# A fused Griffin-style layer on one core: the sums of weight blocks in the gate and up products are made by accumulating transfers

## The chip, the cores and the metric

One core of a Trainium2 chip runs one launch. The metric is the device time in microseconds. A core has five engines that run on their own and meet at semaphores: TensorE (PE, with its weight loads as PEld), VectorE (DVE), ScalarE (ACT), GpSimd (POOL) and SyncE (SP), which in this kernel issues nearly all transfers between the device memory and the on-chip memory.

## The reference, cut to what matters

The layer normalizes x (512 rows of 2048 values), runs a gated recurrence and a sliding-window attention side by side, merges them, adds a cross attention, and ends with a gated feed-forward part and a final norm. The change is in the feed-forward part:

```python
hf = rmsnorm(x, norm_ffn[l])
x = x + (jax.nn.silu(hf @ w_gate[l]) * (hf @ w_up[l])) @ w_down[l]
```

w_gate and w_up are 2048 x 5632, w_down is 5632 x 2048, all in float32.

## The kernel before, in words

Each float32 product is made of three products of a rounded high part and a rest: low x high, high x low, high x high. Weights are therefore split on the chip: ScalarE copies a raw block to its high part (f_hi, line 1499), and VectorE subtracts it from the raw block to get the low part (f_lo, line 2087; the first four on GpSimd, line 557).

Gate and up are computed together as a 2 x 2 block product in the manner of Strassen and Winograd, with seven products in place of eight. The 2048 values that are summed over are halved, and so are the 512 rows of hf. The two halves of w_gate are the blocks b11 and b21, those of w_up are b12 and b22. For each of 11 groups of 512 columns (n = 0 to 10) the seven products p need these right-hand blocks: b11; b11+b12; b11+b12+b22; b22; b12+b22; b21; b11+b12+b22+b21. A block is 1024 x 512 and is worked in four chunks c of 128 x 1024 elements (512 KB), so a group has 28 chunks and chunk i is 28n + 4p + c. For each chunk TensorE does 24 matmuls (line 568 to 570, or 843 to 845 where the sum of two results is wanted in two accumulators).

The raw blocks live in three sets of four slots, f_raw[0..2][c]. SP loads b11, b12, b22 and b21 (quad_load, line 453), each into the slots of one set; the roles of the sets rotate with n (raw_sets). The sums are made in place by VectorE (f_sum, line 2082): one addition of two whole slots for each chunk of p = 1, 2, 4 and 6, two chunks ahead of its f_low in VectorE's order. The semaphore f_t_added counts them, and ScalarE's f_high waits for it. There are three f_hi and three f_lo buffers: f_high(i) waits until TensorE has done chunk i-3 (f_chunk_done), f_low(i) waits for f_high(i), and TensorE waits for f_low(i) (f_lo_ready).

SP's order in a group: after f_lo of chunk 16+c it loads b21 of this group and b11 of the next; after f_lo of chunk 24+c, b12 and b22 of the next; then the two stores of finished activations (store_act, line 480), which wait for ScalarE. In the last group the first four loads of w_down stand where b11 stood. In group 0, VectorE and ScalarE also make the left-hand operands (operand_steps), in a written order between the f_low and f_high calls, from the transposed rows of hf; b12's slots overlap the buffers of the norm before, so its load waits for row_squared and row_scaled.

GpSimd makes the low parts of all earlier weights (line 545), then f_low(0) to f_low(3), and has nothing after them. After the groups comes the down projection of 88 chunks (w_down), whose raw blocks use the slots of one of the sets.

Of the kernel before, what the change touches and what calls it, by code (L numbers as in the profile page):

```python
# [24 lines left out]
P = 128  # L25
# [25 lines left out]
CK = 8  # L51
RING = 4
# [50 lines left out]
def build_trunk(nc, a, out):  # L103

    ctx = ExitStack()
    with ctx:
# [156 lines left out]
        f_hi_ready, f_lo_ready = S("f_hi_ready"), S("f_lo_ready")  # L263
        f_chunk_done, f_t_added = S("f_chunk_done"), S("f_t_added")

# [4 lines left out]
        def raw_sets(n):  # L270

            return ((0, 1, 2), (2, 0, 1), (1, 2, 0))[n % 3]


        load_of = {}
        slot_loads = {}
        for n in range(NQ):
            a_set, b_set, c_set = raw_sets(n)
            for name, x in (("b11", a_set), ("b12", b_set), ("b22", c_set), ("b21", b_set)):
                for c in range(4):  # L280
                    slot_loads[x, c] = slot_loads.get((x, c), 0) + 1
                    load_of[n, name, c] = (x, c, slot_loads[x, c])
# [5 lines left out]
        raw_in = [[S(f"f_raw_in{x}{c}") for c in range(4)] for x in range(3)]  # L288

# [6 lines left out]
        def split_source(i):  # L296

            if i >= 28 * NQ:
                x, c, _ = load_of["down", i - 28 * NQ]
                return f_raw[x][c]  # L300
            n, r, p, c = step(i)
            a_set, b_set, c_set = raw_sets(n)
            return f_raw[(a_set, a_set, a_set, c_set, b_set, b_set, a_set)[p]][c]

        def sums_to(i):

            n, r, p, c = step(i)
            return 16 * n + sum(4 for q in (1, 2, 4, 6) if q < p) + c + 1

# [17 lines left out]

        w_in = a["w_in"].rearrange("l d n -> (l d) n")

        @block.sync  # L330
        def _(sp):
# [110 lines left out]

            w_gate = a["w_gate"].rearrange("l (k p) n -> p (l k) n", p=P)
            w_up = a["w_up"].rearrange("l (k p) n -> p (l k) n", p=P)
            w_down = a["w_down"].rearrange("l (k p) n -> p (l k) n", p=P)

            def quad_load(n, name, c):

                x, slot, _ = load_of[n, name, c]
                w = w_gate if name in ("b11", "b21") else w_up  # L450
                k0 = 2 * c + (0 if name in ("b11", "b12") else CK)
                dst = f_raw[x][slot][:, :].rearrange("p (k n) -> p k n", n=512)
                sp.dma_start(dst, w[:, k0:k0 + 2, n * 512:(n + 1) * 512]).then_inc(raw_in[x][slot], 16)

# [4 lines left out]
            for c in range(4):  # L459
                sp.wait_ge(w_lo_ready, C_XO + 4 + c + 1)  # L460
                quad_load(0, "b11", c)
# [4 lines left out]
            quad_load(0, "b12", 0)  # L466
            sp.wait_ge(S("row_scaled"), 2 * TT)
            for c in (1, 2, 3):
                quad_load(0, "b12", c)
            sp.wait_ge(S("x2_spilled"), 32)  # L470
            sp.wait_ge(S("x2_spilled_late"), 32)
            for c in range(4):
                quad_load(0, "b22", c)

# [61 lines left out]
        @block.gpsimd  # L536
        def _(pool):
            pool.memset(ones[:, :], 1.0).then_inc(S("ones_set"), 1)

            def split_lo(s, v=0, k=0):  # L540

                slot = s % RING
                before(pool, w_hi_ready, s + 1, v, k)
                before(pool, chunk_done, s - RING + 1, v, k)
                pool.tensor_tensor(w_lo[:, slot], w_raw[:, slot], w_hi[:, slot].bitcast(F32),  # L545
                                   ALU.subtract).then_inc(w_lo_ready, 1)

# [12 lines left out]
            for i in range(4):  # L560
                f_low(i)

        @block.tensor
# [583 lines left out]
        def _(act):  # L1147
# [335 lines left out]
            def f_high(i):  # L1483
# [139 lines left out]
        def _(dve):  # L1623
# [440 lines left out]

            def f_sum(i):

                if i >= 28 * NQ:
                    return
                n, r, p, c = step(i)
                if p not in (1, 2, 4, 6):  # L2070
                    return
                a_set, b_set, c_set = raw_sets(n)
                o, other = {1: (a_set, b_set), 2: (a_set, c_set), 4: (b_set, c_set), 6: (a_set, b_set)}[p]
                for name in {1: ("b11", "b12"), 2: ("b22",), 4: (), 6: ("b21",)}[p]:
                    x, slot, count = load_of[n, name, c]
                    dve.wait_ge(raw_in[x][slot], 16 * count)
                if i < 8:
                    dve.wait_ge(f_lo_ready, i - 3)
                if p in (2, 6):
                    dve.wait_ge(f_t_added, sums_to(i - (4 if p == 2 else 16)))  # L2080
                o = f_raw[o][c][:, :]
# [133 lines left out]
            for i in range(2, 28 * NQ + len(DOWN)):  # L2215
                f_sum(i + 2)
                if i == 4:
# [77 lines left out]
```

## Time and profile before

| | us |
|---|---|
| median of 3 runs | 2931.21 (2930.93 to 2933.22) |
| the profiled execution | 2933.35 |
| its span | 2931.5 |
| TensorE busy in the span | 2870.1 |
| VectorE busy | 1351.9 |
| ScalarE busy | 1141.4 |
| GpSimd busy | 618.3 |

The page of the profile gives sums over a program with different stages, so the busy shares alone don't say what a stage is bound by. The view by windows gives the same sums for one stretch, and the timeline gives single instructions with what they waited for. Matmuls of a busy TensorE start 0.23 us apart; the 0.39 us of one overlap with the next. An instruction that issues a transfer isn't counted as busy.

### The profile page before, as it was taken

How to read it: one execution, taken by the hardware profiler on the slowest of the kernel's cores; microseconds unless marked ns; L12 is line 12 of the kernel's file. 1: busy time of each engine (PE TensorE's matmuls, PEld its weight loads, DVE VectorE, ACT ScalarE, POOL GpSimd, SP SyncE). 2: the span in 40 equal slices, each digit the busy share in tenths (PEclk: the TensorE clock that was granted, in tenths of full speed). 3: DMA queues.
4: the chain of work that ended last, by engine and by line, in shares of the span. 5: the costliest groups of instructions: out<-in, count | busy, mean ns of one | idle time of the engine just before them, and what ended most of it. 6: DMA issues, size and time to landing. Idle time of an engine off the chain costs nothing.

```text
span 2931.5 us, 34896 instructions
## 1 busy us (share of the span) xinstructions
PE 2870.1 (98%) x13685; PEld 2388.8 (81%) x13685; DVE 1351.9 (46%) x1618; ACT 1141.4 (39%) x1487; POOL 618.3 (21%) x257
## 2 busy tenths in 40 slices
PE   8999999999999999999999999999999999999998
PEld 7888878788888888878877888888888888888886
DVE  3354555410034300020427977777777775334333
ACT  6443444412244422232335544444444443223223
POOL 6433333244433344444331000000000000000000
PEclk9999999999999999999999999999999999999999
DMA  7422222233322233342223333333332345434442
GB/s 232 121 73 72 72 72 72 60 95 86 103 77 77 85 90 102 106 151 94 87 94 123 130 130 122 130 122 130 127 105 106 123 140 220 146 137 148 151 144 108
DMA packets 330543, 334.05 MB, mean 114 GB/s; under 512 B 26712, under 2 KB 234928, under 8 KB 327344
## 3 DMA queue, kind: packets, MB, share of 16 engines
q1 hardware_dynamic: 329808, 331.95, 34.4%
q8 instruction: 91, 1.49, 0.2%
q10 hardware_dynamic: 608, 0.32, 0.0%
q14 instruction: 36, 0.29, 0.0%
HBM read 311.25 MB, written 20.97 MB: 113 GB/s over the span
## 4 chain that ended last, share of the span: by engine, by line
PE 77%; DVE 3%; ACT 1%; issue 1%; DMA 0%; ACTq 0%; DVEq 0%; SPq 0%
PE psum L568 19%; PE psum L569 19%; PE psum L570 19%; PE psum L843 5%; PE psum L844 5%; PE psum L845 5%; PE psum L889 1%; PE psum L1076 1%; PE psum L787 0%; DVE f_lo L2087 0%; PE psum L768 0%; DVE f_raw L2082 0%; DVE op_lo L1630 0%; PE psum L941 0%; PE psum L777 0%
## 5 line engine op out<-in xcount | busy, mean ns | idle before, releaser
L545 POOL TENSOR_TENSOR w_lo<-w_raw,w_hi 128x1024 fp32r<-128x1024 f32 x248 | 607.7, 2460 | 932.4 <-ACT w_hi L1153 931.2
L1499 ACT ACTIVATE f_hi<-f_raw 128x1024 fp32r<-128x1024 f32 x396 | 419.7, 1061 | 765.3 <-PE psum L570 502.5
L2087 DVE TENSOR_TENSOR f_lo<-f_raw,f_hi 128x1024 fp32r<-128x1024 f32 x392 | 479.7, 1224 | 472.2 <-ACT f_hi L1499 470.9
L568 PE MATMUL psum<-op_hi,w_lo 128*128 128x512 f32 x1216 | 486.8, 400 | 0.0
L569 PE MATMUL psum<-op_lo,w_hi 128*128 128x512 f32 x1216 | 477.6, 393 | 0.0
L570 PE MATMUL psum<-op_hi,w_hi 128*128 128x512 f32 x1216 | 476.8, 392 | 0.0
L1153 ACT ACTIVATE w_hi<-w_raw 128x1024 fp32r<-128x1024 f32 x248 | 257.7, 1055 | 241.4 <-PE psum L570 222.7
L568 PE MATMUL psum<-f_hi,pa_lo 128*128 128x512 f32 x704 | 274.1, 389 | 0.0
L570 PE MATMUL psum<-f_hi,pa_hi 128*128 128x512 f32 x704 | 273.9, 389 | 0.0
L569 PE MATMUL psum<-f_lo,pa_hi 128*128 128x512 f32 x704 | 273.9, 389 | 0.0
L568 PEld LDWEIGHTS psum<-op_hi,w_lo 128*128 128x128 f32 x1216 | 230.8, 190 | 49.2 <-issue 2.4
L570 PEld LDWEIGHTS psum<-op_hi,w_hi 128*128 128x128 f32 x1216 | 230.7, 190 | 49.2
L569 PEld LDWEIGHTS psum<-op_lo,w_hi 128*128 128x128 f32 x1216 | 230.8, 190 | 47.7 <-issue 1.7
L2082 DVE TENSOR_TENSOR f_raw<-f_raw,f_raw 128x1024 f32<-128x1024 f32 x176 | 215.3, 1224 | 3.6 <-DMA f_raw<-in_w_up 3.6
L568 PEld LDWEIGHTS psum<-f_hi,pa_lo 128*128 128x128 f32 x704 | 132.1, 188 | 27.7
L570 PEld LDWEIGHTS psum<-f_hi,pa_hi 128*128 128x128 f32 x704 | 132.1, 188 | 27.6
L569 PEld LDWEIGHTS psum<-f_lo,pa_hi 128*128 128x128 f32 x704 | 132.1, 188 | 27.1
L568 PE MATMUL psum<-f_hi,a_lo 128*128 128x512 f32 x352 | 137.9, 392 | 0.0
L843 PE MATMUL psum<-f_hi,s_lo 128*128 128x512 f32 x352 | 137.0, 389 | 0.2 <-DVE f_lo L2087 0.2
L570 PE MATMUL psum<-f_hi,a_hi 128*128 128x512 f32 x352 | 137.1, 389 | 0.0
L569 PE MATMUL psum<-f_lo,a_hi 128*128 128x512 f32 x352 | 137.0, 389 | 0.0
L845 PE MATMUL psum<-f_hi,s_hi 128*128 128x512 f32 x352 | 136.9, 389 | 0.0
(308 smaller groups left out, 4447.9 us busy)
## 6 DMA issues: line engine op xcount, KB each, us to landing
w_raw<-in_w_in SPq DMA_DIRECT2D x144, 512.0 KB, 3.8
f_raw<-in_w_gate SPq DMA_DIRECT2D x88, 512.0 KB, 4.6
f_raw<-in_w_up SPq DMA_DIRECT2D x88, 512.0 KB, 5.1
f_raw<-in_w_down SPq DMA_DIRECT2D x88, 512.0 KB, 4.7
pa_raw<-act_scratch SPq DMA_DIRECT2D x44, 512.0 KB, 3.9
w_raw<-in_w_out SPq DMA_DIRECT2D x32, 512.0 KB, 3.7
act_scratch<-c SPq DMA_DIRECT2D x22, 512.0 KB, 3.0
w_raw<-in_w_proj_a SPq DMA_DIRECT2D x16, 512.0 KB, 3.8
```

Of the source, the lines that this page charges most:

```text
L545: pool.tensor_tensor(w_lo[:, slot], w_raw[:, slot], w_hi[:, slot].bitcast(F32), ALU.subtract).then_inc(w_lo_ready, 1)
L568: pe.matmul(b[:, 0:n], wl, xh, start=start, stop=False)
L569: pe.matmul(b[:, 0:n], wh, xl, start=False, stop=False)
L570: return pe.matmul(b[:, 0:n], wh, xh, start=False, stop=stop)
L843: pe.matmul(b, lo[:, kt, f], w[0], start=False, stop=False, skip_group_check=True)
L844: pe.matmul(b, hi[:, kt, f], w[1], start=False, stop=False, skip_group_check=True)
L845: return pe.matmul(b, hi[:, kt, f], w[0], start=False, stop=stop, skip_group_check=True)
L889: last = pe.matmul(bank[4 + j][:, x * P:(x + 1) * P], h_nat[:, t % 2, kt * P:(kt + 1) * P], n_diag[:, t % 2, :], start=True, stop=True)
L1153: act.activation(w_hi[:, slot], w_raw[:, slot], ACT.Copy).then_inc(w_hi_ready, 1)
L1499: act.activation(f_hi[i % FR][:, :], split_source(i)[:, :], ACT.Copy).then_inc(f_hi_ready, 1)
L2082: dve.tensor_tensor(o, o, f_raw[other][c][:, :], ALU.add).then_inc(f_t_added, 1)
L2087: dve.tensor_tensor(f_lo[i % FR][:, :], split_source(i)[:, :], f_hi[i % FR][:, :].bitcast(F32), ALU.subtract).then_inc(f_lo_ready, 1)
```

## The change

f_sum is gone. GpSimd issues, after its four f_low, 16 transfers in each group that read a weight block from the device memory and add it onto what is in the slot (accum_op=ALU.add). Each waits for f_lo of the chunk that used the slot last and for the accumulating transfer before it into the same slot number, and increments raw_added[c]; f_high waits for that. The sequence for one group: b11 is loaded into the first set; b12, b22 and b21 are added onto it, for p = 1, 2, 6. b22 is loaded into the second set and b12 added onto it, for p = 4. b21 is loaded into the third set for p = 5, and that set becomes the first one of the next group, while the first becomes the third. The second set stays. b12 and b22 are thus read more often: a group reads 28 blocks of 512 KB from memory where it read 16. SP loads b22 of the next group after chunk 16+c, b11 of the next after 20+c, and b21 of the next after 24+c. The order of adds in GpSimd's queue is p = 1, 2, 6, 4, four chunks each.

```diff
 def raw_sets(n):
-            return ((0, 1, 2), (2, 0, 1), (1, 2, 0))[n % 3]
+            return ((0, 1, 2), (2, 1, 0))[n % 2]
+        BLOCK = ("b11", "b12", "b22", "b22", "b12", "b21", "b21")
+        ADDS = (1, 2, 6, 4)
...
+            sum_set, low_set, next_set = raw_sets(n)
+            for p, x in ((0, sum_set), (3, low_set), (5, next_set)):
                 for c in range(4):
                     slot_loads[x, c] = slot_loads.get((x, c), 0) + 1
+                    load_of[n, p, c] = (x, c, slot_loads[x, c])
+            for j, p in enumerate(ADDS):
+                for c in range(4):
+                    load_of[n, p, c] = (low_set if p == 4 else sum_set, c, len(ADDS) * n + j + 1)
...
+        raw_in = [w_loaded] + [[S(f"f_raw_in{x}{c}") for c in range(4)] for x in (1, 2)]
+        raw_added = [S(f"f_raw_added{c}") for c in range(4)]
...
+        def up_block(n, p, c):
+            w = w_gate if BLOCK[p] in ("b11", "b21") else w_up
+            k0 = 2 * c + (0 if BLOCK[p] in ("b11", "b12") else CK)
+            return w[:, k0:k0 + 2, n * 512:(n + 1) * 512]
...
+            def quad_load(n, p, c):
+                x, slot, _ = load_of[n, p, c]
+                sp.dma_start(raw_pieces(x, slot), up_block(n, p, c)).then_inc(raw_in[x][slot], 16)
...
             for n in range(NQ):
+                if n < NQ - 1:
+                    for c in range(4):
+                        sp.wait_ge(f_lo_ready, 28 * n + 16 + c + 1)
+                        quad_load(n + 1, 3, c)
                 for c in range(4):
-                    sp.wait_ge(f_lo_ready, 28 * n + 16 + c + 1)
-                    quad_load(n, "b21", c)
+                    sp.wait_ge(f_lo_ready, 28 * n + 20 + c + 1)
                     if n < NQ - 1:
-                        quad_load(n + 1, "b11", c)
+                        quad_load(n + 1, 0, c)
                     else:
                         down_load(c)
                 if n < NQ - 1:
                     for c in range(4):
                         sp.wait_ge(f_lo_ready, 28 * n + 24 + c + 1)
-                        quad_load(n + 1, "b12", c)
-                        quad_load(n + 1, "b22", c)
+                        quad_load(n + 1, 5, c)
...
+            def add_block(n, p, c):
+                x, slot, count = load_of[n, p, c]
+                last = {1: 0, 2: 4, 6: 8, 4: 12}[p]
+                pool.wait_ge(f_lo_ready, 28 * n + last + c + 1)
+                if count > 1:
+                    pool.wait_ge(raw_added[c], 16 * (count - 1))
+                pool.dma_start(raw_pieces(x, slot), up_block(n, p, c), accum_op=ALU.add).then_inc(raw_added[c], 16)
+
+            for n in range(NQ):
+                for p in ADDS:
+                    for c in range(4):
+                        add_block(n, p, c)
...
-                    if p in (0, 3, 5):
-                        x, slot, count = load_of[n, {0: "b11", 3: "b22", 5: "b21"}[p], c]
-                        act.wait_ge(raw_in[x][slot], 16 * count)
-                    else:
-                        act.wait_ge(f_t_added, sums_to(i))
+                    x, slot, count = load_of[n, p, c]
+                    act.wait_ge(raw_added[c] if p in ADDS else raw_in[x][slot], 16 * count)
...
-                dve.tensor_tensor(o, o, f_raw[other][c][:, :], ALU.add).then_inc(f_t_added, 1)
...
             for i in range(2, 28 * NQ + len(DOWN)):
-                f_sum(i + 2)
```

## Rows read from the trace of the kernel before

**Rows 1.** The page, its first lines: span, and busy us of each engine.
```profile
span 2931.5 us, 34896 instructions
PE 2870.1 (98%) x13685; PEld 2388.8 (81%) x13685; DVE 1351.9 (46%) x1618; ACT 1141.4 (39%) x1487; POOL 618.3 (21%) x257
```

**Rows 2.** Windows: group 0, a steady group, part of the down projection.
```profile
core 0: us, PE busy (x) PEld busy (x) DVE busy (x) ACT busy (x) POOL busy (x), PEclk, DMA share, GB/s
1569.74:1661.00 91.26, 83.82 (x379) 67.90 (x378) 82.02 (x77) 50.70 (x55) 4.70 (x2) 1.00 0.42 150
2014.67:2090.84 76.17, 76.17 (x346) 63.23 (x345) 58.52 (x50) 35.10 (x34) 0.00 (x0) 1.00 0.34 124
2421.00:2661.00 240.00, 240.00 (x1068) 198.81 (x1067) 92.28 (x79) 75.42 (x74) 0.00 (x0) 1.00 0.45 164
```

**Rows 3.** Waits of TensorE, 1560 to 2440 us: total, times, longest.
```profile
PE psum L843 <- DVE f_lo L2087: 3.8, 4, 2.1
PE psum L568 <- DVE f_lo L2087: 2.0, 2, 1.6
PE psum L568 <- DVE s_lo L2129: 1.6, 1, 1.6
```

**Rows 4.** The page's groups of instructions: busy us, mean ns | idle before.
```profile
L545 POOL TENSOR_TENSOR w_lo<-w_raw,w_hi 128x1024 fp32r<-128x1024 f32 x248 | 607.7, 2460 | 932.4 <-ACT w_hi L1153 931.2
...
L2087 DVE TENSOR_TENSOR f_lo<-f_raw,f_hi 128x1024 fp32r<-128x1024 f32 x392 | 479.7, 1224 | 472.2 <-ACT f_hi L1499 470.9
...
L2082 DVE TENSOR_TENSOR f_raw<-f_raw,f_raw 128x1024 f32<-128x1024 f32 x176 | 215.3, 1224 | 3.6 <-DMA f_raw<-in_w_up 3.6
```

**Rows 5.** The tile f_raw: SP's issues (ns, min/median/max), and all landings.
```profile
L453 SPq DMA_DIRECT2D f_raw<-in_w_gate x88: 367/373/1140, 1526.5 to 2411.3; - x88
...
DMA to landing us min/median/max: 3.4/4.7/16.2
```

**Rows 6.** Timeline, ScalarE, steady state: start, us, instruction, [idle before <- releaser].
```profile
2010.86 1.06 ACT L1499 ACTIVATE f_hi<-f_raw 128x1024 fp32r<-128x1024 f32 x1 [1.66 <-PE psum L845]
2013.58 1.06 ACT L1499 ACTIVATE f_hi<-f_raw 128x1024 fp32r<-128x1024 f32 x1 [1.66 <-PE psum L845]
2016.30 1.06 ACT L1499 ACTIVATE f_hi<-f_raw 128x1024 fp32r<-128x1024 f32 x1 [1.66 <-PE psum L845]
```

**Rows 7.** Timeline, VectorE, the same stretch.
```profile
2010.37 1.22 DVE L2082 TENSOR_TENSOR f_raw<-f_raw,f_raw 128x1024 f32<-128x1024 f32 x1
2011.95 1.23 DVE L2087 TENSOR_TENSOR f_lo<-f_raw,f_hi 128x1024 fp32r<-128x1024 f32 x1 [0.36 <-ACT f_hi L1499]
```

**Rows 8.** Transfers, 2014.67 to 2090.84 us in 40 slices: busy tenths, GB/s.
```profile
DMA  9999970000069999930000160003400000000000
GB/s 356 364 380 386 390 292 3 0 0 0 0 155 398 373 382 392 396 120 0 0 0 0 49 226 0 9 0 129 147 0 0 0 0 0 0 0 0 0 0 0
```

**Rows 9.** Timeline, start of group 0, GpSimd, VectorE, ScalarE, TensorE.
```profile
1573.26 4.70 POOL L557 TENSOR_TENSOR f_lo<-f_raw,f_hi 128x1024 fp32r<-128x1024 f32 x2 [4.35 <-ACT f_hi L1499]
...
1576.76 3.42 DVE L2082 TENSOR_TENSOR f_raw<-f_raw,f_raw 128x1024 f32<-128x1024 f32 x2 [3.63 <-DMA f_raw<-in_w_up]
...
1579.51 1.07 ACT L1499 ACTIVATE f_hi<-f_raw 128x1024 fp32r<-128x1024 f32 x1
1581.35 2.20 ACT L1506 ACTIVATE s_hi<-q_raw 128x1024 fp32r<-128x1024 f32 x2 [0.77 <-DVE q_raw L2119]
...
1585.96 0.47 PE L568 MATMUL psum<-f_hi,s_lo 128*128 128x512 f32 x1 [1.59 <-DVE s_lo L2129]
1608.60 0.47 PE L843 MATMUL psum<-f_hi,sq_lo 128*128 128x512 f32 x1 [2.12 <-DVE f_lo L2087]
1623.36 0.47 PE L843 MATMUL psum<-f_hi,s_lo 128*128 128x512 f32 x1 [0.19 <-DVE f_lo L2087]
```

More of the change, by code:

```diff
@@ L263, in build_trunk @@
         f_hi_ready, f_lo_ready = S("f_hi_ready"), S("f_lo_ready")
-        f_chunk_done, f_t_added = S("f_chunk_done"), S("f_t_added")
+        f_chunk_done = S("f_chunk_done")
         mem_kv_dram = nc.dram_tensor("mem_kv_scratch", [P, 4, 512], F32, kind="Internal").ap()
@@ L270, in raw_sets @@
         def raw_sets(n):
-            return ((0, 1, 2), (2, 0, 1), (1, 2, 0))[n % 3]
+            return ((0, 1, 2), (2, 1, 0))[n % 2]
+        BLOCK = ("b11", "b12", "b22", "b22", "b12", "b21", "b21")
+        ADDS = (1, 2, 6, 4)
         load_of = {}
-        slot_loads = {}
+        slot_loads = {(0, c): C_F // RING for c in range(4)}
         for n in range(NQ):
-            a_set, b_set, c_set = raw_sets(n)
-            for name, x in (("b11", a_set), ("b12", b_set), ("b22", c_set), ("b21", b_set)):
+            sum_set, low_set, next_set = raw_sets(n)
+            for p, x in ((0, sum_set), (3, low_set), (5, next_set)):
                 for c in range(4):
                     slot_loads[x, c] = slot_loads.get((x, c), 0) + 1
-                    load_of[n, name, c] = (x, c, slot_loads[x, c])
+                    load_of[n, p, c] = (x, c, slot_loads[x, c])
+            for j, p in enumerate(ADDS):
+                for c in range(4):
+                    load_of[n, p, c] = (low_set if p == 4 else sum_set, c, len(ADDS) * n + j + 1)
         P2_SET = raw_sets(NQ)[0]
@@ L287, in build_trunk @@
             load_of["down", k] = (P2_SET, c, slot_loads[P2_SET, c])
-        raw_in = [[S(f"f_raw_in{x}{c}") for c in range(4)] for x in range(3)]
+        raw_in = [w_loaded] + [[S(f"f_raw_in{x}{c}") for c in range(4)] for x in (1, 2)]
+        raw_added = [S(f"f_raw_added{c}") for c in range(4)]
         def step(i):
@@ L301, in split_source @@
             n, r, p, c = step(i)
[L302 to L308, printed above, removed]
+            x, c, _ = load_of[n, p, c]
+            return f_raw[x][c]
         block = ctx.enter_context(nc.Block())
@@ L328, in build_trunk, with raw_pieces @@
         w_in = a["w_in"].rearrange("l d n -> (l d) n")
+        w_gate = a["w_gate"].rearrange("l (k p) n -> p (l k) n", p=P)
+        w_up = a["w_up"].rearrange("l (k p) n -> p (l k) n", p=P)
+        def up_block(n, p, c):
+            w = w_gate if BLOCK[p] in ("b11", "b21") else w_up
+            k0 = 2 * c + (0 if BLOCK[p] in ("b11", "b12") else CK)
+            return w[:, k0:k0 + 2, n * 512:(n + 1) * 512]
+        def raw_pieces(x, c):
+            return f_raw[x][c][:, :].rearrange("p (k n) -> p k n", n=512)
         @block.sync
@@ L441, in _ @@
             sp.dma_start(g_row[:, :], a["norm_ffn"].partition_broadcast(P).rearrange("p l d -> p (l d)")).then_inc(S("gain_row_in"), 16)
-            w_gate = a["w_gate"].rearrange("l (k p) n -> p (l k) n", p=P)
-            w_up = a["w_up"].rearrange("l (k p) n -> p (l k) n", p=P)
             w_down = a["w_down"].rearrange("l (k p) n -> p (l k) n", p=P)
[L447 to L453, printed above, removed]
+            def quad_load(n, p, c):
+                x, slot, _ = load_of[n, p, c]
+                sp.dma_start(raw_pieces(x, slot), up_block(n, p, c)).then_inc(raw_in[x][slot], 16)
             def spill(t):
@@ L460, in _ @@
                 sp.wait_ge(w_lo_ready, C_XO + 4 + c + 1)
-                quad_load(0, "b11", c)
+                quad_load(0, 0, c)
             for t in range(TT):
@@ L465, in _ @@
             sp.wait_ge(S("row_squared"), 32)
-            quad_load(0, "b12", 0)
+            quad_load(0, 3, 0)
             sp.wait_ge(S("row_scaled"), 2 * TT)
             for c in (1, 2, 3):
-                quad_load(0, "b12", c)
+                quad_load(0, 3, c)
             sp.wait_ge(S("x2_spilled"), 32)
@@ L472, in _ @@
             for c in range(4):
-                quad_load(0, "b22", c)
+                quad_load(0, 5, c)
             def store_act(n, h):
@@ L2063, in a11_low @@
                     dve.tensor_tensor(A11[1][:, k, f], turned_tiles(j), A11[0][:, k, f].bitcast(F32), ALU.subtract).then_inc(S("a11_ready"), 1)
[L2065 to L2081, printed above, removed]
-                dve.tensor_tensor(o, o, f_raw[other][c][:, :], ALU.add).then_inc(f_t_added, 1)
             def f_low(i):
```

## The prediction

> **What bounds the kernel now.** Read the page's busy shares first: TensorE is busy for 2870.1 us of a span of 2931.5 us [rows 1]. Then cut the gate and up stage into stretches. The stage has 11 column groups (n = 0 to 10), each of 28 chunks: seven products p of four chunks c, where chunk i = 28n + 4p + c. A whole group in the steady state takes 76.17 us and TensorE is busy in all 76.17 of it; VectorE has 58.52, ScalarE 35.10, GpSimd 0.00, and the granted clock is 1.00 [rows 2]. So one chunk is 76.17/28 = 2.72 us, and nothing that only relieves VectorE can shorten ten of the eleven groups. The down projection after it is equally full (240.00 of 240.00) [rows 2]. The first group is different: in the 91.26 us from the first gate chunk, TensorE is busy 83.82, VectorE 82.02 [rows 2]. The missing 7.44 us is, in the view of waits, TensorE waiting for VectorE: 3.8 + 2.0 us for f_lo, 1.6 us for the operand s_lo [rows 3]. That is the whole prize of taking work from VectorE here: 7.4 us, or 0.25% of the run.
>
> I call a difference of 0.2% (5.9 us) the least that this kernel's measurement can tell from none. The sum is made against the profiled execution, 2933.35 us (its span of 2931.5 and 1.85 around it), which lies 2.1 us above the median of 2931.21; the difference is then put on the median.
>
> **What is removed.** 176 additions at L2082, 1.224 us each, 215.3 us of VectorE's time, 16 a group [rows 4]. In groups 1 to 10 VectorE is idle 17.65 us of 76.17 anyway and TensorE never waits for it: worth 0. In group 0 it may give back part of the 7.44 us. SP issues 12 loads a group instead of 16. The later load times cost nothing: b11 of group n+1 used to be issued after f_lo of chunk 16+c and is now after chunk 20+c, eight chunks (21.8 us) before its chunk, of which 2.3 us are the split's; the slowest load of this tile landed in 16.2 us [rows 5]. b22 and b21 go out 24 chunks ahead, and the first four down loads also keep eight chunks. On SP's queue, the two act stores wait as before for the staged tiles, and the loads behind them have the same first release, chunk 16 of the next group.
>
> **What is added: 16 accumulating transfers a group, issued by GpSimd.** GpSimd has no other work in this stage, so nothing of its own queues behind them; but the transfers queue behind each other, in the order p1, p2, p6, p4. Each of p1, p2 and p4 is released by f_lo of the chunk four places earlier in the same slot, and f_hi waits for its landing; p6's have twelve chunks more.
>
> The deadline. f_hi starts every 2.72 us, released by TensorE finishing the chunk three before [rows 6]; f_lo ends 2.32 us after f_hi's start (2010.86 to 2013.18: the f_lo row starts at 2011.95 and lasts 1.23) [rows 6, 7]. From the end of f_lo(i) to the undisturbed start of f_hi(i+4) there are 4 x 2.72 - 2.32 = 8.56 us. If it is later, TensorE still has two chunks, 5.44 us, before it needs f_lo of that chunk, which takes 2.32: 3.12 us of slack. Two links (p1, then p2) come in a row, then p3, which needs no sum, gives the slack back, then p4. With a latency L from f_lo to landing, a group therefore stalls by max(0, 2(L - 8.56) - 3.12) + max(0, L - 8.56 - 3.12): nothing up to L = 10.1 us.
>
> The latency. No accumulating transfer and no transfer from GpSimd stands in this trace, so it is bounded. A stretch with back to back loads of this very shape moves 356 to 398 GB/s with the engines at 90% or more [rows 8]; at 390 GB/s, 524,288 bytes take 1.35 us. The fastest landing, 3.4 us [rows 5], leaves about 2.05 us beside the bytes. An accumulate has to bring two operands to the adder, so I take 2 x 1.35 = 2.70 us for the bytes; the lower end is 1.35 (the second read hides), the upper 4.05 (read, read and write each take a pass). GpSimd's share in writing the descriptors lies between SP's issue of the same block, 0.37 us, and a pass of GpSimd over the same 128x1024 tile, 2.46 us [rows 4, 5]. No row is nearer to one end; I take the middle, 1.4. L = 2.05 + 2.70 + 1.4 = 6.2 us, between 3.8 and 8.6. All of that is within 10.1.
>
> The rate. Sixteen transfers of 2.70 are 43.2 us. From the end of f_lo(0) to the last moment for p4's last block (chunk 19) there are 19 x 2.72 - 2.32 + 3.12 = 52.5 us. With about 3 us for the last one's latency beside its bytes and 2.7 for the two act stores in between, the place is lost when one add costs more than (52.5 - 5.7)/16 = 2.93 us, whether it is GpSimd or the transfer engines that set the pace. 2.70 is below it, but by a hair: this is where the prediction hangs. The plain loads mostly come after chunk 16, where no add is issued, and per group the engines have to carry 14 plain blocks (12 loads, 2 stores) x 1.35 + 16 x 2.70 = 62.1 us of 76.2. Steady state: 0, with 4.05 kept for the range.
>
> By the Trainium skill (Collectives: The Full Stack, "The bandwidth ceiling") an add in the transfer engines is free in itself and costs because two sources are read: half the rate of a copy. The trace has no add to confirm it; by its rule this transfer takes 2 x 1.35 = 2.70 us, and from its figure of about 31 GB/s an engine, halved, over 16 engines, I estimate 2.1 us. Both would leave the steady state at 0. The row of 390 GB/s is 24 GB/s an engine, below the page's figure.
>
> **Group 0.** GpSimd first finishes f_lo(2) and f_lo(3), at 1573.26 + 4.70 = 1577.96 [rows 9], and only then issues p1's first block; it lands at about 1584.1. Before, VectorE did that sum from 1576.76 on and f_hi(4) ran at 1579.51 [rows 9]. Now f_hi(4) runs 1584.1 to 1585.2, and behind it in ScalarE's queue stands s_hi, which no longer starts at 1581.35 [rows 9] but at 1585.2; its first half is done at 1586.3, f_lo(4) at 1586.4, s_lo's first half at 1587.6. So chunk 4 starts at 1587.6 instead of 1585.96 [rows 9]: 1.6 us lost. From there the same walk, in queue order and without the additions (1.14 us apart each) on VectorE, follows ScalarE and VectorE through q_raw, sq, s4 and s: adds land every 2.70 us (1586.8, 1589.5, 1592.2, 1594.9, ...), which delays f_hi(7) and (8) by under 1 us; five additions that stood on VectorE between 1585.96 and 1608.60 are gone (5.7 us), but f_lo then waits for ScalarE's halves of the operands instead. It comes to chunk 10 at about 1608.1 instead of 1608.60 and chunk 15 at about 1622.4 instead of 1623.36, after which TensorE is full. Net gain 1.0 us; with L = 3.8 it is 3, with L = 8.6 it is -1.5.
>
> The sum: 2933.35 - 1.0 + 0 = 2932.3 us against the profiled run, and 2931.2 - 1.0 = 2930.2 us against the median.
>
> **Rivals.**
> (a) The transfer engines set the pace: three passes a transfer, 4.05 us. For it: 2.70 already fills 43.2 of the 43.5 us in which the 16 are released. Against it: a plain load has a read and a write as well, and they evidently overlap within 1.35. Price: 16 x 4.05 = 64.8, plus 3, less 52.5, is 15.3 us a group; times 11 is 168 us: 3099 us. It decides above 2.93 us an add, and the loads of the next group would still fit. 20%.
> (b) GpSimd sets the pace: writing descriptors for 512 KB (and two reads each) takes longer than the chunk. For it: the same tile costs this engine 2.46 us where VectorE takes 1.22, so it is slow work there; against it, SP issues the block in 0.37. At 3.5 us an add, 16 x 3.5 + 3 - 52.5 = 6.5 us a group, +72 us: 3003 us; at two tile passes (4.9) +318. Middle taken: 3.9 us, +142 us: 3073 us. 20%.
> Beside this one, the Trainium skill (SBUF — State Buffer, "Who interferes with whom") says that GpSimd can't write descriptors while a two-port VectorE operation holds the shared port; VectorE would be busy 58.5 - 18.3 = 40.2 of 76.2 us here. Were all of it blocking, 1.4 us of writing would become 1.4/0.47 = 3.0 us, at the threshold, as an estimate. The page expects no such block from two-input tensor operations, which these are; no row here shows either.
> (c) The pace fits, but latency does not: L = 12 (completion behind queued traffic; single loads took up to 16.2 us). 3.8 + 0.3 = 4.1 us a group, +44 us: 2975 us. 9%.
> (d) Faster: L near 4, the operand chain speeds up as much as VectorE is relieved and more than 5.9 of the 7.44 us come back: 2925 us. Against it, chunk 4 alone starts no earlier than now. 6%.
> My forecast, 0 in the steady state and within 5.9 us in all: 45%.
>
> **How the numbers follow.** The forecast is the likeliest single case, own range 2926 to 2936. Slower is a sum of three mechanisms, 20 + 20 + 9 = 49%; faster 6%; same 45%. Low end 2926 leaves 5% below it. The high end covers (a) at 3099 and (b)'s middle, and leaves out (b) from about 3.9 us an add: 3130, with 15% above.
>
> **What would show it.** Right: adds at GpSimd landing in 5 to 8 us, TensorE busy in all of 76.2 us in groups 1 to 10, VectorE near 40 a group, no L2082, f_hi still released by TensorE; chunk 4 of group 0 one or two us later. (a): transfer engines at 90% or more through chunks 0 to 19, with f_hi(16 to 19) waiting for the transfer and GpSimd's issues short. (b): GpSimd's issues above 2.9 us back to back. (c): gaps in GpSimd's issue, engines not full, f_hi waiting at chunks 8 and 16. The prediction is wrong if a group takes more than 76.5 us.

## The result and the profile after

The changed kernel takes 2937.26 us (median of 20 runs, 2934.99 to 2940.01) beside 2932.95 us for the kernel before in as many runs: a ratio of 1.0016, 95% interval 1.0010 to 1.0022, some 4.3 us more (2.9 to 6.5 by the interval). The forecast was 1.0 us less. Its profiled execution took 2936.05 us, with a span of 2934.2.

The page's first lines, its line on the queue of GpSimd's transfers (packets, MB, share of the 16 engines' time), and the line on the landing of GpSimd's transfers (the last number is the median in us from issue to landing):

```profile
span 2934.2 us, 34892 instructions
...
PE 2871.4 (98%) x13685; PEld 2390.1 (81%) x13685; DVE 1158.1 (39%) x1442; ACT 1141.4 (39%) x1487; POOL 830.5 (28%) x433
...
q0 software_dynamic: 47872, 92.29, 18.1%
...
f_raw<-in_w_up POOLq DMA_DIRECT2D x132, 512.0 KB, 7.5
```

VectorE lost 194 us of work against [rows 1], and TensorE has no less to do. GpSimd's busy time rose by 212 us: unlike SP's, its instructions that issue a transfer are counted as busy, 176 of them at 1.20 us each. Where the 4.3 us come from shows in the same stretches as in [rows 2]. Windows of the changed kernel: group 0 (from its own first chunk, 1.8 us earlier by the clock of this execution), 28 chunks of steady work, a whole group from one copy of its first product to the next, the down projection.

```profile
core 0: us, PE busy (x) PEld busy (x) DVE busy (x) ACT busy (x) POOL busy (x), PEclk, DMA share, GB/s
1567.90:1662.00 94.10, 85.99 (x382) 70.59 (x381) 63.19 (x61) 50.69 (x55) 26.56 (x20) 0.95 0.91 217
2014.67:2090.84 76.17, 76.17 (x346) 63.23 (x345) 41.56 (x35) 35.46 (x35) 19.25 (x16) 1.00 0.91 203
1750.15:1828.13 77.98, 77.98 (x354) 64.74 (x353) 42.26 (x35) 36.16 (x37) 19.25 (x17) 1.00 0.91 202
2421.00:2661.00 240.00, 238.53 (x1059) 196.67 (x1058) 87.89 (x74) 73.39 (x74) 0.00 (x0) 1.00 0.48 173
```

The steady groups are what was forecast: full. The share of the transfer engines went from 0.34 to 0.91 and TensorE did not wait. (Where the engines are saturated, below, this share reads 1.04 to 1.13, so 0.91 isn't 91% of what they can do.) A whole group takes 77.98 us, before and after, not the 76.17 of 28 chunks: a chunk is 12 matmuls (not the 24 of the description above) that start 0.227 us apart, and the 16 transposes of the activations of the group before (turn_act) take the other 1.81.

Group 0 and the stretch where the down projection begins are where TensorE stands. Its waits from 1560 to 2450 us (before the change [rows 3] are all, up to 2450 too):

```profile
PE psum L592 <- DVE s_lo L2131: 7.0, 1, 7.0
PE psum L867 <- DVE f_lo L2089: 2.0, 3, 0.9
PE psum L592 <- DVE f_lo L2089: 0.6, 1, 0.6
```

To compare runs whose earlier stages differ by up to 4 us, I take three lengths from each trace: group 0 from the start of f_hi(0) to the copy of the first product in group 1 (c<-psum, ScalarE), nine group lengths between the same copy in group 1 and in group 10, and from there to the end of the span. Each length is from one profiled execution. Before: 1562.27 to 1671.78, to 2373.60, to 2931.5. After: 1560.46 to 1672.17, to 2373.99, to 2934.2.

| kernel | group 0 | nine groups, copy 1 to copy 10 | from there on | ratio to before (95%) |
|---|---|---|---|---|
| before | 109.51 | 701.82 | 557.9 | |
| changed | 111.71 | 701.82 | 560.2 | 1.0016 (1.0010 to 1.0022) |
| changed, timed again (c_after) | 112.68 | 701.81 | 560.2 | 1.0016 (1.0007 to 1.0025) |
| e1_interleave | 108.49 | 701.82 | 560.5 | 1.0004 (0.9995 to 1.0013) |
| e2_act_first | 111.92 | 701.82 | 558.0 | 1.0011 (1.0002 to 1.0020) |
| e3_hold | 114.27 | 701.81 | 560.2 | 1.0025 (1.0015 to 1.0035) |
| e4_plain | 109.37 | 701.82 | 560.1 | 1.0002 (0.9993 to 1.0012) |
| e5_both | 107.95 | 701.82 | 558.0 | 0.9995 (0.9986 to 1.0004) |
| e8_fill | 112.01 | 701.82 | 561.4 | 1.0018 (1.0009 to 1.0027) |
| e9_order | 109.42 | 701.82 | 558.2 | 1.0000 (0.9991 to 1.0009) |
| e10_hybrid | 112.10 | 701.82 | 558.0 | 1.0005 (0.9996 to 1.0014) |
| e11_b21 | 112.81 | 701.82 | 560.1 | 1.0019 (1.0010 to 1.0028) |
| e12_p4first | 107.90 | 701.82 | 558.0 | 0.9994 (0.9985 to 1.0003) |

So the change costs 2.2 us in group 0 (3.2 in the repeat), nothing in the nine group lengths after it, and 2.3 us where the down projection begins: 4.5 in all, beside 4.3 between the medians. The span grew by only 2.7 since the stages before the change were 1.8 us quicker in this execution.

**Group 0.** The timeline of its start in the changed kernel, GpSimd, SP, ScalarE, VectorE, TensorE. It answers to [rows 9].

```profile
1571.46 4.70 POOL L567 TENSOR_TENSOR f_lo<-f_raw,f_hi 128x1024 fp32r<-128x1024 f32 x2 [4.36 <-ACT f_hi L1520]
1576.11 5.04 POOL L580 DMA_DIRECT2D f_raw<-in_w_up  x4
...
1569.66 3.30 SPq L461 DMA_DIRECT2D f_raw<-in_w_up  x4
1573.63 2.11 SPq L461 DMA_DIRECT2D f_raw<-in_w_gate  x4
...
1585.93 1.06 ACT L1520 ACTIVATE f_hi<-f_raw 128x1024 fp32r<-128x1024 f32 x1 [8.10 <-DMA f_raw<-in_w_up]
...
1588.23 2.35 DVE L2131 TENSOR_TENSOR s_lo<-q_raw,s_hi 128x1024 fp32r<-128x1024 f32 x2
...
1589.55 0.77 PE L592 MATMUL psum<-f_hi,s_lo 128*128 128x512 f32 x1 [6.99 <-DVE s_lo L2131]
```

The first add goes out at 1576.11 and f_hi(4) starts at 1585.93, 9.8 us later: it shares the engines with SP's plain loads of b22 and b21, issued from 1569.66 and from 1573.63 on. (Which of them count, e11_b21 shows below.) s_hi and s_lo stand behind f_hi(4), so TensorE waits 6.99 us where it waited 1.59 [rows 9]. The wait's releaser is named VectorE's s_lo; the cause is three steps back, a transfer. And the granted clock falls during the idle time. Windows, changed kernel:

```profile
1575.00:1581.00 6.00, 6.00 (x37) 5.33 (x37) 2.36 (x2) 1.64 (x4) 6.00 (x5) 1.00 1.04 381
1587.00:1589.00 2.00, 0.00 (x0) 0.00 (x0) 1.91 (x2) 1.88 (x2) 0.39 (x1) 0.50 1.09 260
1593.00:1595.00 2.00, 2.00 (x6) 1.52 (x6) 2.00 (x3) 2.00 (x3) 0.71 (x1) 0.50 1.12 205
1597.00:1599.00 2.00, 2.00 (x10) 1.65 (x9) 1.26 (x2) 1.73 (x2) 0.12 (x1) 1.00 1.13 207
```

Columns as before; the last three are clock, engine share and GB/s. With plain loads in the mix the engines move 381 GB/s, with adds alone 205 to 207: 524,288 bytes every 2.53 us, against 1.35 for a plain block [rows 8]. From about 1585, some 2.5 us into the wait, to 1595 TensorE has the lower of its two clocks (0.50, 1.2 GHz).

**The end.** Timeline of the last group, SP, ScalarE and TensorE, changed kernel:

```profile
2414.37 8.53 SPq L494 DMA_DIRECT2D f_raw<-in_w_down  x4
2423.01 2.59 SPq L524 DMA_DIRECT2D pa_raw<-act_scratch  x5
...
2428.38 1.06 ACT L1603 ACTIVATE pa_hi<-pa_raw 128x1024 fp32r<-128x1024 f32 x1 [4.41 <-DMA pa_raw<-act_scratch]
...
2431.89 0.50 PE L867 MATMUL psum<-f_hi,a_lo 128*128 128x512 f32 x1 [0.86 <-DVE f_lo L2089]
2441.20 0.47 PE L592 MATMUL psum<-f_hi,pa_lo 128*128 128x512 f32 x1 [0.61 <-DVE f_lo L2089]
```

The same five pa_raw loads in the kernel before:

```profile
2412.25 3.09 SPq L514 DMA_DIRECT2D pa_raw<-act_scratch  x5
```

They stand behind the first four down loads on SP's queue, and the change moved those from chunk 16+c to chunk 20+c. The loads left 10.8 us later, pa_hi waited 4.41 us at the head of ScalarE's queue, and f_hi of the next chunks stood behind it. Against the kernel before, f_lo falls 2.3 us behind there by the ninth down chunk and stays so to the end; TensorE's two gaps show 1.5 us of that, since the gap is counted from the modelled end of a matmul and the first after it is slower.

### The profile page after: what moved, and what is told of

The parts are those of the page before. It is cut to its first block, busy times and chain, and to the rows that moved or that the text cites. A ratio compares the mean times of both kernels' runs of the same rounds, so it can differ in the third digit from the quotient of the medians.

```text
span 2934.2 us, 34892 instructions
## 1 busy us (share of the span) xinstructions
PE 2871.4 (98%) x13685; PEld 2390.1 (81%) x13685; DVE 1158.1 (39%) x1442; ACT 1141.4 (39%) x1487; POOL 830.5 (28%) x433
## 3 DMA queue, kind: packets, MB, share of 16 engines
q0 software_dynamic: 47872, 92.29, 18.1%
## 4 chain that ended last, share of the span: by engine, by line
PE 77%; DVE 2%; DMA 1%; ACT 1%; issue 0%; POOL 0%; ACTq 0%; SPq 0%; DVEq 0%
PE psum L592 19%; PE psum L594 19%; PE psum L593 19%; PE psum L867 5%; PE psum L868 5%; PE psum L869 5%; PE psum L913 1%; DMA f_raw<-in_w_up 1%; PE psum L1100 1%; PE psum L811 0%; PE psum L792 0%; DVE f_lo L2089 0%; DVE op_lo L1651 0%; PE psum L965 0%; PE psum L801 0%
## 5 line engine op out<-in xcount | busy, mean ns | idle before, releaser
L580 POOL DMA_DIRECT2D f_raw<-in_w_up x132 | 159.2, 1228 | 542.4 <-DVE f_lo L2089 521.6
L868 PE MATMUL psum<-f_lo,s_hi 128*128 128x512 f32 x352 | 136.9, 389 | 0.0
```

The costliest lines, as they stand in the source:

```text
L580: pool.dma_start(raw_pieces(x, slot), up_block(n, p, c), accum_op=ALU.add).then_inc(raw_added[c], 16)
L868: pe.matmul(b, hi[:, kt, f], w[1], start=False, stop=False, skip_group_check=True)
```

## The experiments

**The changed kernel again**, timed beside the next three.

> The changed kernel itself, timed beside the others. Every theory: 1.0016 of the kernel before (1.0010 to 1.0022), some 4.3 us, of which its trace shows 2.2 us in group 0, 0.0 in groups 1 to 10 and 2.3 us where the down projection begins.

Measured: 1.0016, group 0 112.68. Between these two executions group 0 differs by 1.0 us, the end by 0.1 at most.

**e1_interleave: the adds of p1 behind their own f_low.**

```diff
-            for i in range(4):
-                f_low(i)
...
+            for c in range(4):
+                f_low(c)
+                add_block(0, 1, c)
...
+                    if n == 0 and p == 1:
+                        continue
```

> GpSimd issues p1's add for slot c right behind f_low(c), not behind all four f_low. Theory A (the first add is late because it stands behind f_low(3) and then meets the plain loads of b22 and b21): the first two adds go out some 8 us earlier, chunk 4's f_hi no longer waits for a transfer, TensorE's wait of 7.0 us before chunk 4 falls to under 2 us and its clock stays at 1.00; 6 to 8 us less than the changed kernel, 2 to 4 us less than before. Rival B (the operand chain hf_raw, q_raw, s_hi, s_lo sets chunk 4 anyway): the wait stays above 5 us and the time within 1.5 us of the changed kernel.

Measured: 1.0004, 3.4 us under the changed kernel's median beside it (2933.91 and 2937.28); group 0 108.49, 1.0 less than before. The wait before chunk 4 is gone. Theory A holds in its place and is too large in its size, because part of the waiting moved to the next sums. TensorE's waits in e1_interleave up to 2500 us; 5.1 us of them lie in group 0, before chunks 7 to 10, the rest where the down projection begins:

```profile
PE psum L869 <- DVE f_lo L2091: 5.9, 4, 2.6
PE psum L594 <- DVE f_lo L2091: 0.6, 1, 0.6
```

**e2_act_first: pa_raw's loads ahead of the down loads.**

```diff
             for n in range(NQ):
                 if n < NQ - 1:
...
+                else:
+                    for m in range(AR):
+                        act_load(m)
...
-            for m in range(AR):
-                act_load(m)
```

> In the last group SP issues the five loads of pa_raw ahead of the first four down loads. Theory C (these five loads stood behind a wait that moved from chunk 16+c to 20+c, so pa_hi waits 4.4 us and holds up f_hi behind it): the pa_raw loads go out near 2413 us as before the change, ScalarE does not wait for them, TensorE has no gap near 2432 and 2441; 2.3 us less than the changed kernel. Rival D (the transfer engines are full of adds there, so the loads are late wherever they are issued): under 0.8 us less, and ScalarE still waits 3 us or more for pa_raw.

Measured: from group 10 to the end 558.0 us, the 557.9 of before; 2935.80 us, 1.5 under the changed kernel. The time shows less than the trace's 2.3, within the interval. The waits of ScalarE from 2400 to 2450 us have no line with a transfer any more. First the changed kernel (its repeat), then e2_act_first:

```profile
ACT f_hi L1520 <- PE psum L869: 13.1, 8, 1.7
ACT f_hi L1520 <- PE psum L594: 7.7, 3, 4.3
ACT pa_hi L1603 <- DMA pa_raw<-act_scratch: 4.4, 1, 4.4
ACT sig L1587 <- DVE c L2173: 1.1, 1, 1.1
```

```profile
ACT f_hi L1521 <- PE psum L870: 16.3, 11, 1.7
ACT f_hi L1521 <- PE psum L595: 8.2, 5, 3.5
```

Theory C holds, and rival D falls.

**e3_hold: both sets of plain loads held until p1's add has landed.**

```diff
-            quad_load(0, 3, 0)
             sp.wait_ge(S("row_scaled"), 2 * TT)
-            for c in (1, 2, 3):
+            for c in range(4):
+                sp.wait_ge(raw_added[c], 16)
                 quad_load(0, 3, c)
...
             for c in range(4):
+                sp.wait_ge(raw_added[c], 16)
                 quad_load(0, 5, c)
```

> In group 0, SP holds the plain loads of b22 and b21 for slot c until p1's add into slot c has landed. If sharing the transfer engines with these loads makes the first add slow (9.8 us from issue to f_hi), it lands in 6 to 7 us, chunk 4 starts 3 us earlier and the whole is 3 to 5 us faster than the changed kernel. If it is the place of the add behind f_low(3) alone, its landing stays near 9.8 us and the time within 1 us.

Measured: 1.0025, slower by 2.8 us than the changed kernel's 2937.28. Its timeline, GpSimd, ScalarE, SP and TensorE:

```profile
1575.72 5.04 POOL L581 DMA_DIRECT2D f_raw<-in_w_up  x4
...
1581.82 1.06 ACT L1521 ACTIVATE f_hi<-f_raw 128x1024 fp32r<-128x1024 f32 x1 [4.37 <-DMA f_raw<-in_w_up]
...
1581.82 10.86 SPq L461 DMA_DIRECT2D f_raw<-in_w_up  x4
...
1585.44 0.77 PE L593 MATMUL psum<-f_hi,s_lo 128*128 128x512 f32 x1 [3.25 <-DVE s_lo L2132]
```

The add alone takes 6.1 us from issue to f_hi, in place of 9.8: sharing the engines was worth 3.7 us, as the first theory said, and 6.1 is near the 6.2 that the prediction had worked out. But the held loads then met the later adds. Counted from f_hi(0), chunk 4's f_lo came 3.7 us sooner than in the changed kernel, chunk 15's 0.7 us sooner, and chunk 16's 3.8 us later: its f_hi waited 5.5 us for p4's add, issued while b21's loads were still landing. TensorE's waits for f_lo in group 0 came to 4.5 us, against 1.1. The mechanism was right, and the expected gain was wrong: the adds of p2 and p4 took it back.

**e4_plain: the same transfers without adding** (the sums are left out, so the output is another).

```diff
-                pool.dma_start(raw_pieces(x, slot), up_block(n, p, c), accum_op=ALU.add).then_inc(raw_added[c], 16)
+                pool.dma_start(raw_pieces(x, slot), up_block(n, p, c)).then_inc(raw_added[c], 16)
```

> The 176 transfers of GpSimd copy their block instead of adding it (the sums are left out; everything is issued and waited for as in the changed kernel). If an add costs more of the transfer engines than a copy because it brings two operands, a steady group's engine share falls from 0.91 to about 0.55 (30 plain blocks of 1.35 us in 76.2), the median landing from 7.5 to 5 us, GpSimd's issue stays at 1.2 us, and group 0 gets back 3 us or more since chunk 4 no longer waits 7 us. If the share comes from GpSimd's queue itself and not from the adding, share and landing stay near 0.9 and 7.5.

Measured: 1.0002, group 0 109.37. Its queue line and landing from the page, then its steady window:

```profile
q0 software_dynamic: 25344, 92.29, 10.5%
...
f_raw<-in_w_up POOLq DMA_DIRECT2D x132, 512.0 KB, 4.6
```

```profile
2014.67:2090.84 76.17, 76.17 (x346) 63.24 (x345) 41.94 (x35) 35.15 (x34) 11.58 (x16) 1.00 0.68 201
```

For the same 92.29 MB the queue's share falls from 18.1% to 10.5% (a factor of 1.72), packets from 272 to 144 a transfer, the landing from 7.5 to 4.6 us. GpSimd's time per issue falls too, from 19.25/16 = 1.20 to 11.58/16 = 0.72 us, which I had expected to stay. The share in a steady group falls to 0.68, not to the 0.55 of my count. Chunk 4 still waited 5.7 us, as its transfer still shared the engines with the plain loads; the gain of 2.3 us in group 0 came at the following chunks.

**e6_delay1 and e7_delay2: the deadline.** In groups 1 to 10 the adds of p1, p2 and p4 are released one or two chunks later.

```diff
-                pool.wait_ge(f_lo_ready, 28 * n + last + c + 1)
+                pool.wait_ge(f_lo_ready, 28 * n + last + c + 1 + (1 if n and p != 6 else 0))
```

(2 in place of 1 for the second.)

> In groups 1 to 10 each add of p1, p2 and p4 waits for the f_lo of one chunk more. This tests the deadline that the prediction worked out: an add takes about 7.7 us from f_lo to landing and then 2.3 to the next f_lo, 10.0 us a link; links now come every three chunks (8.16 us) instead of every four (10.88). Three links in p1 and p2 are then 5.5 us late less 3.1 of slack, two in p4 3.7 less 3.1: 3 us a group, 30 us in all. If there is much more room than that deadline says, it is 0 to 5 us.

> The same with two chunks more: a link every two chunks (5.44 us) that takes 10.0. Four links in p1 and p2 are 18.2 us late less 3.1, two in p4 9.1 less 3.1: 21 us a group, about 210 us in all. With much more room than worked out: under 60 us.

Measured (two runs each): 2969.72 us and 3140.68 us beside 2933.79 for the kernel before; less the 4.3 us of the change itself that is 31.6 and 202.6, where 30 and 210 were expected. TensorE's waits, one chunk later from 1680 to 2420 us, then two chunks later from 1680 to 2620:

```profile
PE psum L867 <- DVE f_lo L2089: 21.0, 13, 2.7
```

```profile
PE psum L867 <- DVE f_lo L2089: 110.5, 53, 5.2
PE psum L592 <- DVE f_lo L2089: 25.8, 11, 3.3
```

The nine group lengths grew from 701.82 to 730 us and to 887. In the first, 21 of these 29 us are gaps before matmuls, and the link of 10.0 us, the period of 2.72 and the slack of 3.12 are borne out. In the second the gaps are 136 us of the 203; the mean granted clock over its nine groups was 0.94, which is worth up to 53 us more. The sum knew of no clock, so that it came so near the second is in part luck. What both show is that the adds had less than one chunk, 2.72 us, of room.

**e8_fill: is the half clock paid for?** Spare matmuls before chunk 4.

```diff
+                if i == 4:
+                    spare = A11[0][:, 0:2, :].rearrange("p k f -> p (k f)")
+                    for _ in range(28):
+                        pe.matmul(o[:, 0], A11[0][:, 0, 0:P], spare, start=True, stop=True)
```

> TensorE runs 28 spare matmuls (6.4 us, constants in, into a bank that chunk 4 then overwrites) between chunks 3 and 4 of group 0, where it waits 7 us for s_lo. If the idle time lowers the clock and the half clock from 1587 to 1595 us costs work, the granted clock stays at 1.00, chunk 4 starts when it did and the run is 2 to 3 us shorter than the changed kernel. If the half clock is hidden because the adds set the pace there anyway, the time is the same within 1 us.

Measured: 1.0018, group 0 112.01, no less than the changed kernel. TensorE's rows and the window after them:

```profile
1586.48 6.51 PE L1078 MATMUL psum<-a_hi 128*128 128x512 f32 x28
1593.80 0.50 PE L592 MATMUL psum<-f_hi,s_lo 128*128 128x512 f32 x1 [0.82 <-DVE s_lo L2135]
```

```profile
1582.00:1600.00 18.00, 16.84 (x73) 13.12 (x71) 9.45 (x9) 6.52 (x7) 5.62 (x5) 1.00 1.10 260
```

The clock stayed at 1.00 and nothing was won: TensorE's waits for f_lo in group 0 grew from 1.1 us in the changed kernel to 3.0. With the 0.8 us before s_lo and the 6.5 us of spare matmuls TensorE lacked real work for 10.3 us there, against 8.1 in the changed kernel: the 2.2 us that the higher clock saved came back as waiting. Over these chunks the adds and the operand chain set the pace, and the half clock ran in their shadow. The first theory (2 to 3 us) falls. The stretch after the nine groups was 1.2 us longer than in the changed kernel: pa_hi waited 5.7 us there in place of 4.4, and TensorE behind it 2.1 in place of 0.9. Why the loads took longer in that execution is open.

**e5_both: e1_interleave and e2_act_first together** (both diffs above).

> Both edits that helped alone: p1's add of a slot right behind its f_low in group 0, and pa_raw's loads ahead of the first down loads. They act in different places, so by theory A and C they add: 2.2 to 4 us in group 0 and 2.3 us at the end less than the changed kernel, about 2931.5 us beside 2933 for the kernel before (0.9995, range 0.999 to 1.000). If the gain of the one is eaten by the other's place, no more than 3.5 us in all.

Measured: 2931.90 us beside 2933.10 for the kernel before, 0.9995 (0.9986 to 1.0004): 1.2 us under the kernel before, where the changed kernel is 4.3 over it, and not told apart from before. The lengths add: group 0 107.95, the rest 558.0.

**e9_order, e10_hybrid and e11_b21: b21's loads later.** The first adds this to e5_both:

```diff
             for c in range(4):
+                sp.wait_ge(f_lo_ready, 12 + c + 1)
                 quad_load(0, 5, c)
```

The third has it alone. The second has it with pa_raw's loads first and group 0's p1 summed by VectorE as before the change (b12 is loaded into the second set for that, b22 after the sum):

```diff
+                if i < 6:
+                    c = i - 2
+                    dve.wait_ge(raw_in[1][c], 16)
+                    dve.wait_ge(f_lo_ready, c + 1)
+                    o = f_raw[0][c][:, :]
+                    dve.tensor_tensor(o, o, f_raw[1][c][:, :], ALU.add).then_inc(S("f_first_sum"), 1)
...
```

> e5_both, and SP also holds group 0's four loads of b21 (needed at chunk 20) until f_lo of chunk 12+c. Theory E (what is left in group 0 is the transfer engines: in e1_interleave TensorE waited 5.9 us before chunks 7 to 10 for sums whose adds shared them with eight plain loads of 1.35 us): the waits shrink by 3 to 5 us, and the run ends 3 to 5 us under e5_both, 0.9980 to 0.9990 of before. Rival F (the operand chain between VectorE and ScalarE sets those chunks): the waits move to other releasers and the time is within 1 us of e5_both.

> Group 0's p1 is summed by VectorE as before the change (b12 loaded into the second set, b22 loaded there after the sum), the other 172 adds stay transfers; with pa_raw's loads first and b21 held. By theory E chunk 4 starts as in the kernel before (1.6 us of wait) and four adds of 2.53 us are gone from the crowded stretch; VectorE has 12 sums fewer than before: 0.9978 to 0.9990 of before, no slower than e9_order. If VectorE's four sums (4.9 us) delay q_raw and s_lo as they did before, it is 1 to 2 us slower than e9_order.

> The changed kernel with only b21's four loads of group 0 held until f_lo of chunk 12+c. If the first add is slow since these loads stand before it at the transfer engines (9.8 us to f_hi; 6.1 us where all eight loads were held), chunk 4 starts about 3 us earlier, without the late b22 that cost e3_hold its gain: 2 to 3 us less than the changed kernel. If b22's loads alone make it slow, under 1 us.

Measured: 1.0000, 1.0005 and 1.0019: none brought the gain that was expected. Their traces say more than their times.

In e11_b21 the first add takes 6.2 us from issue to f_hi, as in e3_hold, though b22's four loads were under way as in the changed kernel (GpSimd, then ScalarE):

```profile
1579.60 5.04 POOL L581 DMA_DIRECT2D f_raw<-in_w_up  x4
1585.80 1.06 ACT L1521 ACTIVATE f_hi<-f_raw 128x1024 fp32r<-128x1024 f32 x1 [4.46 <-DMA f_raw<-in_w_up]
```

So it is b21's four loads, issued just before the add, that made it 3.6 us slower, and b22's cost it nothing. TensorE's wait before chunk 4 fell from 7.0 to 3.3 us.

In e9_order the same loads are out of the way of p2's adds. f_hi of chunks 8 and 9, first in e5_both, then in e9_order:

```profile
1596.83 1.06 ACT L1523 ACTIVATE f_hi<-f_raw 128x1024 fp32r<-128x1024 f32 x1 [2.98 <-DMA f_raw<-in_w_up]
1600.86 1.06 ACT L1523 ACTIVATE f_hi<-f_raw 128x1024 fp32r<-128x1024 f32 x1 [2.97 <-DMA f_raw<-in_w_up]
```

```profile
1592.01 1.06 ACT L1524 ACTIVATE f_hi<-f_raw 128x1024 fp32r<-128x1024 f32 x1 [0.76 <-DMA f_raw<-in_w_up]
1594.55 1.06 ACT L1524 ACTIVATE f_hi<-f_raw 128x1024 fp32r<-128x1024 f32 x1 [1.48 <-DMA f_raw<-in_w_up]
```

All four wait for their add. With plain loads of the other queue under way the adds land 4.03 us apart, without them 2.54 apart: the 1.5 us more for each are near the 1.35 of a plain block. TensorE's waits before chunks 7 to 11 fell from 4.8 to 1.9 us, and f_lo of chunk 10 came 3.6 us sooner. That is theory E, and not F, as far as these chunks go. But b21's loads were then issued beside p4's adds, and these came late. f_hi of chunks 16 and 19 in e9_order:

```profile
1618.16 1.06 ACT L1524 ACTIVATE f_hi<-f_raw 128x1024 fp32r<-128x1024 f32 x1 [4.83 <-DMA f_raw<-in_w_up]
...
1630.61 1.06 ACT L1524 ACTIVATE f_hi<-f_raw 128x1024 fp32r<-128x1024 f32 x1 [3.37 <-DMA f_raw<-in_w_up]
```

The loads were taken out of one crowd and put in another. e10_hybrid, 2.2 us slower than e9_order, did what its second branch said: VectorE's four sums delay s_lo as before the change (a wait of 1.6 us before chunk 4).

**e12_p4first: e5_both with p4's adds ahead of p6's.**

```diff
-        ADDS = (1, 2, 6, 4)
+        ADDS = (1, 2, 4, 6)
```

> e5_both with GpSimd's order p1, p2, p4, p6 in place of p1, p2, p6, p4: p6's adds, needed at chunk 24, no longer go ahead of p4's, needed at 16. If group 0's waits before chunks 8 to 11 and f_hi's waits near chunk 17 are the transfer engines being full (share 1.10 from 1582 to 1620 us) of work that isn't due yet, group 0 falls from 107.95 us by 1 to 3 us and the run by as much below e5_both (0.9985 to 0.9993 of before). If it's only p1's and p2's own adds at 2.53 us each, group 0 stays within 0.5 us. Groups 1 to 10 stay at 0 either way.

Measured: 0.9994 (0.9985 to 1.0003), group 0 107.90, within 0.05 of e5_both. The engines are emptier after the change of order, e5_both first (share 1.11), then e12_p4first (0.59), each from about 40 us after its f_hi(0):

```profile
1604.50:1624.50 20.00, 17.44 (x70) 13.91 (x70) 15.98 (x14) 14.74 (x15) 7.44 (x7) 0.91 1.11 201
1600.00:1620.00 20.00, 17.40 (x70) 13.89 (x70) 15.97 (x14) 14.64 (x15) 5.55 (x6) 0.91 0.59 103
```

TensorE's waits in it are no shorter for that, 4.6 us where e5_both has 4.7. So p6's adds, which are issued only after chunk 8's f_lo, are not what TensorE waits for there. By e9_order it is b21's loads that stretch the waits before chunks 7 to 10. No run here moved them to a place where they cost nothing.

## Why the prediction was wrong

**The steady state: right.** Nine group lengths, 701.82 us before and after. The estimate of 2.70 us for an add (two operands, each a plain pass) was measured at 2.53, under the threshold of 2.93 that had been worked out. GpSimd's issue was taken as 1.4 us and is 1.20. The latency was taken as 6.2; the first add took 6.1 to 6.2 from issue to f_hi without b21's loads beside it, and all adds 7.6 to landing in the median. The deadline formula was tested from the other side by e6_delay1, and with the reservation above by e7_delay2. Rivals (a), (b) and (c), which together had 49%, did not happen in these groups; what (c) names, a landing behind other traffic, is what happened to the first adds of group 0. The kernel became slower for reasons outside the steady groups.

Two of the prediction's readings were off without hurting the sum. It took 76.17 us for a whole group, which is 28 x 2.72 and leaves the transposes out. So its sign of being wrong, a group above 76.5 us, would have pointed at the kernel before as well (77.98). And it called 5.9 us the least that can be told from none; the measured 4.3 us has an interval of 2.9 to 6.5 us, which excludes zero.

What the Trainium skill states (Collectives: The Full Stack, "The bandwidth ceiling"), that an add halves the rate because two sources are read, agrees with the trace in its size: 2.53 against 1.35 us is a factor of 1.87. No run here shows that the second read is the reason, and the 2.1 us that the prediction estimated from the page's figure per engine was too short. The Trainium skill's page "SBUF — State Buffer" ("Who interferes with whom") expects no block of descriptor writing from two-input VectorE operations, and the trace shows none: GpSimd's issues stood at 1203 ns in the minimum and the median while VectorE was busy 41.56 of 76.17 us.

**Group 0: the failed step is the first landing.** The step "it lands at about 1584.1" used a latency with the engines to itself. In the 6.5 us before the add SP had issued eight plain loads, and the last four, 4 x 1.35 = 5.4 us of the engines' time, shared the engines with it. SP's loads there are the same in number before the change, and then no later transfer was needed at once. The add was 3.7 us later than without them, shown by e3_hold and, with b21's four loads alone, by e11_b21; its own time from release to landing replaced a sum of 1.2 us on VectorE. The walk said chunk 4 would be 1.6 us late, and it was 5.4 late against f_hi(0) (29.09 us after it, 23.69 before). The gain that was forecast for the later chunks is real: TensorE's waits for f_lo in group 0 fell from 5.8 us to 1.1. That is 4.7 us, against 5.4 lost before chunk 4. The other 1.5 us of the net +2.2 are a remainder; the stretch at the lower clock is their likely place, though e8_fill shows that keeping the clock up doesn't bring them back. The forecast was -1.0.

**The end: the step was not worked out.** "The first four down loads also keep eight chunks" is true, and is not the question: what stands behind a moved wait on its queue is. Behind these four stand five pa_raw loads that had no such wait ahead of them. The term was set at 0 and measured 2.3 us, and e2_act_first gives it back whole.

The two terms measured 2.2 and 2.3 us, where the forecast had -1.0 and 0.

## What to carry to other kernels

When a wait on an in-order queue is moved, list the instructions behind it on that queue before asking whether the moved ones are in time; the moved ones were, and the five behind them weren't. When a sum or copy becomes a transfer, take its latency with the traffic that is under way at that very moment, above all at the start of a stage, where prefetches come in a burst; holding the prefetches back only moves the collision to the next sums, while issuing the first adds as soon as their own slot is free took the first wait away. A transfer that shares the engines with another queue's loads doesn't wait for all of them; it gets its turn between them, and each turn costs it their time. A kernel whose TensorE is full for ten groups out of eleven gives nothing for a relieved VectorE: the best version of the change, 0.9994 (0.9985 to 1.0003), can't be told from the kernel before.

## What the runs showed of the hardware

- An accumulating transfer of 512 KB in rows of 2 KB costs the transfer engines 1.87 times a plain one by the bytes moved (207 against some 390 GB/s), 1.72 times by the queue's share of their time (18.1% against 10.5%). It is counted as 272 packets against 144 from the same queue, and takes GpSimd 1.20 us to issue against 0.72 for a copy of the same block. The soonest landed 5.7 us after its issue.
- Two queues take turns on the engines: adds landed 4.03 us apart with plain loads of SP's queue under way, 2.54 without (e5_both, e9_order).
- Transfers at 203 GB/s (a share of 0.91) beside a full TensorE cost it nothing: 76.17 us busy of 76.17. ScalarE's f_hi started late in these groups 16 times, by up to 3.4 us, without a wait of TensorE.
- Spare matmuls during a 7 us gap kept the granted clock at 1.00 where it fell to 0.50 for 10 us without them, and won no time, because TensorE wasn't what those chunks waited for.
